# Gate and up of the second layer in pairs of 64-column matmuls, a separate buffer for the first output-projection tile, and bulk loads moved behind the next tile's rows

## The reference, cut to what matters

```python
for l in range(2):
    h = modulate(x, shift, scale)                    # adaLN: m[0..5] from silu(c) @ w_ada + b_ada
    p = h @ w_in                                     # keys, queries, low-rank parts, gates
    o_a = window attention; o_b = dense latent attention
    y = (sigmoid(g_a) * (o_a @ w_oa) + sigmoid(g_b) * (o_b @ w_ob)) @ w_out
    x = layer_norm(ALPHA * x + m[2] * y)             # ln1
    h = modulate(x, m[3], m[4])
    # expert choice: 16 experts, each takes the top 128 latent tokens (and 32 context tokens in layer 1)
    for e in range(16):
        yg = (silu(xg @ w_gate[e]) * (xg @ w_up[e])) @ w_down[e] * affinity
        z[idx] += yg
    x = layer_norm(ALPHA * x + m[5] * z)             # ln2
```

## Time and profile before

| | |
|---|---|
| median of 3 runs | 4308.33 us (4306.9 to 4308.96) |
| profiled execution | 4310.35 us, its span 4308.7 us |
| TensorE busy, mean granted clock | 4090.0 us (95%), 0.975 |
| VectorE, ScalarE, GpSimd busy | 1885.0, 1062.0, 252.1 us |
| layer 1, start of the output projection | 1252 us from the span's start |
| layer 1, experts | 1490 to 2331 us |
| layer 2, start of the output projection | 3398 us |
| layer 2, experts | 3584 to 4260 us |

### The profile page before, as it was taken

How to read it: one execution, slowest core, us unless ns; L and a number is a source line. 1 busy time by engine, 2 the same in 40 slices (tenths; PEclk the granted TensorE clock), 3 DMA queues, 4 the chain that set the end, 5 groups by cost and what they waited for, 6 DMA issues and landing times.

```text
span 4308.7 us, 72009 instructions
## 1 busy us (share of the span) xinstructions
PE 4090.0 (95%) x27662; PEld 2880.1 (67%) x27662; DVE 1885.0 (44%) x4142; ACT 1062.0 (25%) x2431; POOL 252.1 (6%) x261
## 2 busy tenths in 40 slices
PE   8999999999999799999999999999999977999995
PEld 4555667655544588888886555667644436999994
DVE  2235566532225433333334444666533354444444
ACT  1225555400012211111112324555401121010101
POOL 0000000000000011111111000000000000101012
PEclk9999999999999899999999999999999998999997
DMA  5111000322244798888886221000211437999994
GB/s 206 52 58 41 16 16 15 97 79 80 68 152 157 270 285 269 269 266 263 269 262 187 74 75 46 9 16 15 69 44 44 164 120 230 322 320 328 321 327 162
DMA packets 567756, 653.16 MB, mean 152 GB/s; under 512 B 20245, under 2 KB 494997, under 8 KB 567561
## 3 DMA queue, kind: packets, MB, share of 16 engines
q1 hardware_dynamic: 548600, 605.26, 43.6%
q0 software_dynamic: 18960, 45.23, 4.4%
HBM read 579.57 MB, written 70.86 MB: 151 GB/s over the span
## 4 chain that ended last, share of the span: by engine, by line
PE 83%; DVE 3%; DMA 1%; issue 1%; SPq 1%; DVEq 1%; ACT 0%; POOL 0%; POOLq 0%; ACTq 0%
PE PS L675 44%; PE PS L1178 9%; PE PS L679 7%; PE PS L835 7%; PE PS L1005 5%; PE PS L893 3%; PE PS L886 2%; PE PS L813 2%; PE PS L1172 1%; DVE arena L1515 1%; SPq L383 1%; PE PS L899 1%; PE PS L690 1%; DVE arena L1957 1%; DVEq L1962 0%
## 5 line engine op out<-in xcount | busy, mean ns | idle before, releaser
L675 PE MATMUL PS<-arena 128*128 128x160 f32 (+4 forms) x11296 | 2237.2, 360 | 13.7 <-DVE arena L1515 3.8
L675 PEld LDWEIGHTS PS<-arena 128*128 128x128 f32 x11296 | 1604.8, 191 | 623.3 <-issue 566.7
L1515 DVE TENSOR_TENSOR arena<-arena,PS 128x256 f32<-128x256 f32 (+3 forms) x668 | 293.9, 448 | 1074.9 <-ACT arena L1488 576.4
L1515 DVE TENSOR_TENSOR arena<-arena 128x1024 f32<-128x1024 f32 (+9 forms) x814 | 585.1, 736 | 338.5 <-PE PS L675 234.3
L679 PEld LDWEIGHTS PS<-arena 128*128 128x128 f32 (+1 forms) x3074 | 372.6, 142 | 288.9 <-issue 199.4
L679 PE MATMUL PS<-arena 128*128 128x128 f32 (+1 forms) x3074 | 473.2, 281 | 45.0 <-DVE arena L1515 13.5
L1178 PE MATMUL PS<-arena 128*64 128x256 f32 x3584 | 393.8, 380 | 3.2 <-issue 3.2
L835 PE MATMUL PS<-arena 96*128 96x512 f32 (+1 forms) x800 | 364.0, 537 | 16.0 <-issue 14.1
L1488 ACT ACTIVATE arena<-PS 128x160 f32<-128x160 f32 (+1 forms) x256 | 74.5, 291 | 1208.5 <-PE PS L675 1184.8
L1178 PEld LDWEIGHTS PS<-arena 128*64 128x64 f32 x3584 | 276.3, 137 | 116.3 <-issue 12.6
L1005 PE MATMUL PS<-arena 128*128 128x512 f32 x576 | 262.0, 610 | 10.5 <-POOL arena L2171 5.3
(11 more groups left out here) (200 smaller groups left out, 2001.8 us busy)
## 6 DMA issues: line engine op xcount, KB each, us to landing
arena<-in_w_exp_gate SPq DMA_DIRECT2D x128, 1024.0 KB, 6.0
arena<-in_w_exp_up SPq DMA_DIRECT2D x128, 1024.0 KB, 8.5
arena<-in_w_exp_down SPq DMA_DIRECT2D x128, 1024.0 KB, 7.6
arena<-in_w_ada SPq DMA_DIRECT2D x24, 2048.0 KB, 16.6
arena<-in_w_in SPq DMA_DIRECT2D x32, 512.0 KB, 5.3
h_transposed<-arena SPq DMA_DIRECT2D x20, 512.0 KB, 4.3
x_mid<-arena SPq DMA_DIRECT2D x18, 512.0 KB, 2.9
moe_sum<-arena SPq DMA_DIRECT2D x18, 512.0 KB, 3.4
```

What stands on the lines that cost most here:

```text
L675: m = pe.matmul(o, lt, rh, start=start and i == 0, stop=stop and i == n - 1)
L1515: return dve.tensor_tensor(o, x, y, op)
```

## The change

1. In layer 2, each gate or up matmul with a 128x128 weight block becomes two with 128x64, which write partitions 0 to 63 and 64 to 127 of the same bank. Layer 1 keeps its form.
2. The first tile of the output projection has its own staging buffer `mst1`. GpSimd fills it as soon as that tile's chunk of the last merge block is summed (count `7 * NCH[l] + ...`), and the second tile goes to `mst` without a wait for TensorE. TensorE waits for the last `mrg` but one, and its wait for `modT_cp` stands before the second tile.
3. SyncE's ring loads and layer 1's two modulation loads are issued inside `step1` of the first tile, after the second tile's rows are asked for (`between`).
4. The unused indirect gather moves to the start of the program with a small target; SyncE waits for it before the first merge weights of layer 1, and VectorE's wait, memset and drain for it go.

```diff
+        mst1 = at(O + 23040, KD, P)
+        first_rows = at(O + 27648, P)
+        first = at(O + 27776, 2).bitcast(U32)
...
                 sp.wait_ge(*s("mxW", 16 * NPAIR[l]))
+                if l == 0:
+                    sp.wait_ge(G["warm"], 16)
                 weights(0)
...
-                for c in ahead:
-                    ring_load(0, c)
+                def ahead_loads():
+                    for c in ahead:
+                        ring_load(0, c)
+                    if l == 0:
+                        ada_load(1, 0, adC[0], 0)
+                        ada_load(1, 6, adC[1], 1)
                 if l == 0:
-                    ada_load(1, 0, adC[0], 0)
-                    ada_load(1, 6, adC[1], 1)
...
-                        step1(t, t, False)
+                        step1(t, t, False, None if t else ahead_loads)
...
-                    tiles(sp, step1, TL[l][0])
+                    step1(TC, TC, False, ahead_loads)
+                    with sp.Fori(TC + 1, TT - 1) as t:
+                        step1(t, t, False)
+                    step1(TT - 1, TT - 1, True)
...
-                pe.wait_ge(*s("mrg", 8 * NCH[l]))
+                pe.wait_ge(*s("mrg", 8 * NCH[l] - 1))
...
-                            m = pe.matmul(PS[:, h, :], mst[:, k, :], w_o[:, k, h * 512:(h + 1) * 512], start=k == 0, stop=k == KD - 1)
+                            m = pe.matmul(PS[:, h, :], (mst1 if isinstance(n, int) and n == 0 else mst)[:, k, :], w_o[:, k, h * 512:(h + 1) * 512], start=k == 0, stop=k == KD - 1)
...
-                    pe.wait_ge(G["modT_cp"], 1)
                     for t in range(TT):
+                        if t == 1:
+                            pe.wait_ge(G["modT_cp"], 1)
                         y_step(t)
...
-                    pe.wait_ge(G["modT_cp"], 3)
                     for t in range(TL[l][0], TC + 2):
+                        if t == TL[l][0] + 1:
+                            pe.wait_ge(G["modT_cp"], 3)
                         y_step(t)
...
-                            m = mms(PS[:, 3 + f % 2, h * N:(h + 1) * N],
-                                    [(ring[:, (f // 2) * 2 + h, k, (f % 2) * P:(f % 2 + 1) * P], xgT[:, k, 0:N]) for k in range(KD)])
+                            w = ring[:, (f // 2) * 2 + h, :, (f % 2) * P:(f % 2 + 1) * P]
+                            if l == 0:
+                                m = mms(PS[:, 3 + f % 2, h * N:(h + 1) * N], [(w[:, k, :], xgT[:, k, 0:N]) for k in range(KD)])
+                                continue
+                            for k in range(KD):
+                                for g in range(2):
+                                    m = pe.matmul(PS[g * 64:(g + 1) * 64, 3 + f % 2, h * N:(h + 1) * N], w[:, k, g * 64:(g + 1) * 64], xgT[:, k, 0:N],
+                                                  start=k == 0, stop=k == KD - 1)
...
-                if l == 0:
-                    dve.memset(icur[:, 0:1], 0)
-                    dve.drain()
...
-                if l == 0:
-                    dve.wait_ge(G["warm"], 16)
...
+            pool.memset(first, 0)
+            pool.drain()
+            pool.nop(nofuse=True)
+            pool.indirect_dma_start(out=first_rows[0:CAP_C, :], out_offset=None, in_=a["ident"],
+                                    in_offset=bass.IndirectOffsetOnAxis(ap=first[0:CAP_C, 0:1], axis=0)).then_inc(G["warm"], 16)
...
-                pool.wait_ge(*s("mrg", 8 * NCH[l]))
 
                 def take(t):
                     n = t - tl
+                    if isinstance(n, int) and n == 0:
+                        for c in range(2):
+                            pool.wait_ge(*s("mrg", 7 * NCH[l] + (c if l else 1)))
+                            pool.tensor_copy(mst1[:, c * 4:c * 4 + 4, :], mrgT[:, c * 4:c * 4 + 4, t * P:(t + 1) * P]).then_inc(s["mst"], 1)
+                        return
+                    if isinstance(n, int) and n == 1:
+                        pool.wait_ge(*s("mrg", 8 * NCH[l]))
                     for c in range(2):
-                        if not (isinstance(n, int) and n == 0):
+                        if not (isinstance(n, int) and n == 1):
                             pool.wait_ge(*s("y" if c else "y_mid", n))
...
-                if l == 0:
-                    pool.wait_ge(*s("zs", 1))
-                    pool.nop(nofuse=True)
-                    pool.indirect_dma_start(out=snap[0:CAP_C, 0:2, :].rearrange("p a b -> p (a b)"), out_offset=None, in_=a["x"][0],
-                                            in_offset=bass.IndirectOffsetOnAxis(ap=icur[0:CAP_C, 0:1], axis=0)).then_inc(G["warm"], 16)
-                with pool.Fori(tl + 1, TT) as t:
+                take(tl + 1)
+                with pool.Fori(tl + 2, TT) as t:
                     take(t)
```

## The result

The changed kernel takes 4280.11 us (median of 4 runs, 4276.98 to 4283.01) beside 4307.61 us for the kernel before (4 runs, 4306.0 to 4308.96): 27.5 us less, ratio 0.9933, 95% interval [0.9922, 0.9945]. The prediction was 4280.0 us. The profiled execution took 4276.98 us, its span is 4275.3 us and the mean granted clock 0.978.

The account below looks back on a forecast made before the run. TensorE's matmuls take 83% of the time, so only shortening its streams or idle stretches pays. Terms 10.5 + 5.8 + 12.0 = 28.3 us off 4308.33 give 4280.0 us; range 4274 to 4294, the forecast's own 4277 to 4286.

Parts of the forecast that it names:

- layer 1, merge to tile 3: Layer 1's output projection: without stops and clock drop, the staged tiles start earlier, saving 10.5 us.
- layer 2, merge to tile 3: Layer 2's output projection: earlier first tile, and no wait for the second tile's rows, saving 5.8 us.
- layer 2's experts: Gate/up: 4096 instructions of 112.4 ns become pairs of 109.5, the middle of 109.2 (attention's) and 109.9, saving 12.0 us.
- Waits behind it keep their cover: Layer 2's experts: faster pairs expose no waits, since ring loads are refilled an expert ahead.
- No cost for the weight loads: Layer 2's gate/up: twice as many half-width weight loads run beside matmuls, as in attention, so nothing more was counted.
- Rival (d): Gate/up weight loads run without cover, adding 109 ns a pair, 447 us in all: 4727 us; chance 0.01.
- by 0.8 us: Layer 1's projection: VectorE, after the late x1 store, is free at 1294.5, before tile 2's product ends at 1295.3.
- Just not hidden: 0.5 us: Layer 2's projection: after the late x1 store, VectorE is free 0.5 us after tile 2's product ends.
- Rival (a): The x1 store behind the bulk decides: bulk 5 us later, projection gains 6.3 and 0.8 us, total 4289; chance 0.14.
- Rival (b): Layer 2's gate/up pairs gain nothing, the weight path staying at 112.4 ns: gain 16.3 us, 4292; chance 0.09.
- Rival (c): Layer 2's expert loop outgrows TensorE's sequencer: 12 jumps at 5.8 us each add 70 us, 4350; chance 0.08.
- Rival (e): An unseen cost, such as a slowed first gather, cancels the gains: within 0.2% of before; chance 0.05.

Follow-up runs that it names:

- run 7: The changed kernel with layer 1's gate and up also in 64-column pairs (160 moving columns): 4298.65 us.
- run 4: The changed kernel without the 64-column pairs, so first-tile staging and moved loads together: 4295.48 us, ratio 0.9968 to the kernel before.
- run 8: The changed kernel with two experts in each body of TensorE's layer 2 loop, 2528 matmul and load instructions instead of 1264: 4320.2 us.
- run 10: The changed kernel itself measured once more, unedited: 4281.45 us, ratio 0.9943 to the kernel before.
- Run 6: The changed kernel with ScalarE's scaling of a tile's x1 moved one step later, behind its copy of the router sums: 4278.74 us.
- run 5: The changed kernel with the bulk loads dealt out in four parts, each behind the stores of one of the first four tiles: 4277.45 us.
- run 9: The changed kernel with bulk loads in four parts behind the first four tiles' stores and ScalarE's scaling behind its router-sum copy: 4274.64 us.
- run 1: The kernel before with only layer 2's gate and up in 64-column pairs: 4296.03 us, ratio 0.9973.
- run 2: The changed kernel without the pairs and with SyncE's bulk loads at their old place, so staging alone: 4301.95 us, ratio 0.9992 to the kernel before.
- run 3: The kernel before with only the bulk loads moved behind the second tile's rows: 4309.54 us, ratio 1.0004.

## Why the prediction was right, step by step

**Where the 28 us came from.** In the profiles, by differences between the same events before and after:

| | predicted | measured |
|---|---|---|
| layer 1, merge to tile 3 | 10.5 | 10.9 |
| layer 2, merge to tile 3 | 5.8 | 3.8 |
| layer 2's experts | 12.0 (10.2 to 13.2) | 11.6 |
| sum | 28.3 | 26.3 |
| all other stretches | 0 | 7.1 |

The 7.1 us lie where nothing was changed: 2.9 before layer 1's merge ends (the attention loop's gaps are 2.76 and 2.83 us instead of 2.97 and 2.95, with the clock's drops behind them), 2.0 between layer 1's tile 3 and the first down product of its experts, 2.4 from there to the end of layer 2's merge, and -0.3 behind layer 2's tile 3 (they add to 7.0, the rest is rounding). Most of it is the choice of the two executions: the profiled one of before is 2.7 us above its median, that of after 3.1 below, 5.9 together. Medians differ by 27.5, where 28.3 was forecast. That the forecast met the median to 0.1 us is luck: it started from 4308.33 us, the median of three runs of the kernel before, which four runs put at 4307.61, and the touched places gave 26.3 us in the profiles, 2.0 less than the sum.

**The pairs.** Right in kind: the price fell from 112.4 to attention's end of the bounds, 109.2 ns a pair, not to the middle. At 109.2 the term is 13.2; one wait for down weights (1.2 us) and a first expert that gained only 0.46 us (30.79 to 30.33) took it back to 11.6. The sentence "Waits behind it keep their cover" was wrong by this one wait. Alone, the pairs gave 11.1. The reason given was weaker than the price: that load and matmul are both busy for all of the 28.78 us was read as "the load is as long as the matmul". At 160 columns both are busy for the whole piece as well (34.97 of 34.97 us), and there the pairs cost time (run 7). What carried the forecast was attention's 109.2 ns, measured in the same shape.

**No cost for the weight loads.** Shown: 27.78 of 27.95 us beside matmuls. Rival (d) is out. It rested on the Trainium skill's rule in "TensorE: Matmul & The Clock Gate", Part 3, that a weight load overlaps matmuls in flight only if it goes to other rows, and the trace disagrees with that rule at 512 loads in 27.95 us. The same Part's paragraph on the mechanism also lets a load run ahead that goes to the background weight buffer. The trace agrees with that reading, but does not show which buffer a load used.

**Layer 1's projection.** In the change's first profile each step came as worked out. The stop is gone, tile 0 took 13.94 us (14.1 taken), tile 1 follows after 1.41, tile 2 after 15.4 us. The store, reckoned 42.2 us after tile 0's start, released VectorE at 42.25. What was hidden "by 0.8 us" was over by 0.61 us, through ScalarE. That this cost so little was luck of one execution: the other four profiles with the bulk at this place (runs 4, 7, 8 and 10) have 1.84 to 3.16 us there, and gain 9.0, 8.9, 8.2 and 9.1 us at the checkpoint instead of 10.9.

**Layer 2's projection, the term that was mis-sized: 5.8 taken, 3.8 measured.** Counted from tile 0's start, tiles 1 and 2 hold to 0.5 us. The prediction had written "I am wrong if [...] tile 3 gains less than tile 2 by more than 1 us", and this sign came: tile 2 gained 6.6 us, tile 3 3.8. VectorE's wait, expected under 7 us, was 8.89. The failed step is "VectorE free at 3441.1; tile 2's product ends at 3440.6. Just not hidden: 0.5 us." It asks only when VectorE can empty PSUM for tile 3. But ScalarE scales the rows of x1 that VectorE has just written, and in its queue behind that stands the copy of router sums, without which TensorE can't do the router's last product, the transposes and tile 3. On this way the same store costs about 1.2 us more than reckoned (5.33 us from VectorE's start to tile 3 instead of 2.8 + 1.3), and the store itself was 1.0 us later. Run 6 shows the first (3.71 us without ScalarE's queue in between), run 5 the whole (47.2 without the wait). Rival (a) was thus partly true. Against the checkpoints of run 9 (47.0 and 47.1), which has no such wait, the late store costs 0.3 and 3.2 us in the change's first profile and 2.1 and 2.3 in its second. Over all five profiles with the bulk at this place it is 3.5 to 6.3 us for both layers together, and the projection gains 11.9 to 14.7 us, where the sum had 16.3.

**Rival (b), no gain from pairs**: refuted by run 1. **Rival (c), the body that is too long**: did not happen, and its mechanism is real in this loop: 1264 instructions run without a stop, 2528 with one at every jump (run 8). That attention's stop, with 1889, has the same cause is likely but was not tried; no run shortened that body. The Trainium skill's 2048 instructions for TensorE ("Runtime: NRT & Kernel Launch", Instruction fetch mechanics) agrees with the two bodies of experts; attention's 1889 matmuls and loads alone would fit in it, and yet that loop stops. My price of 5.8 us a jump was low for this loop: 7. **Rival (e)**: nothing stood against the gain. The first real gather, which it named, has 3.69 us in layer 1's chain of waits, instead of 5.47 before.

**What the parts are worth alone.** The prediction costed parts 2 and 3 as a sum, 16.3 us. Runs 2 to 4 show that they are no sum: 5.2 us (interval including 0) for the staging and nothing measurable for the loads alone, 11.7 together.

## What to carry to other kernels

When a store or load is moved behind a bulk, follow its landing through every engine's in-order queue up to the engine that sets the end: the first consumer may have room and the one behind it none. Deal a bulk out in parts behind the small transfers that have a deadline. Halve a f32 weight block of 128 columns into pairs only where the full form costs more per moving column than it does at longer shapes (128 columns here, 112.4 ns against 109.3 by the rate); at 160 columns it costs time. A busy share of 100% for the weight loads is no sign of it. Read a margin of under 1 us from more than one execution before calling a wait hidden.

## What the runs showed of the hardware that was not expected

- A pair of 64-column f32 matmul instructions costs 109.2 ns at 128 moving columns (27.95 us for 512 instructions; 28.02 to 28.15 us, up to 110.0 ns, in runs 1 and 5 to 8), where one full instruction costs 112.4; at 160 columns 139.5 against 136.6.
- The stop at a jump back took 2.56 to 3.15 us in attention's loops over all kernels (DMA share 0.03 to 0.05 where it was read) and 4.7 to 5.25 us in the doubled expert loop (DMA share 1.04 to 1.10). Whether the busy queues or the longer body make the difference was not tried.
- A stop of 7.43 us brought the granted clock to 0.65 over the 8 us behind it, a mix of 1.2 and 2.4 GHz. Staging alone therefore made layer 2's projection 3.3 us longer although no work was added. The length of a stop alone did not decide: behind 3.27 us in run 4 the granted clock was 0.63 over 8 us, behind 3.38 us at the same place in the change it was 1.00.
